# RMS norms of a two-layer trunk on one core: half of the sums by one fp32 product with a matrix of ones

## The reference

```python
def _rmsnorm(x, gain):
    xf = x.astype(jnp.float32)
    y = xf * lax.rsqrt(jnp.mean(xf * xf, axis=-1, keepdims=True) + EPS)
    return (y * gain.astype(jnp.float32)).astype(x.dtype)

def _swiglu(h, w_in, w_out):
    g, u = jnp.split(h @ w_in, 2, axis=-1)
    return (jax.nn.silu(g) * u) @ w_out
```

## Time and profile before

| | |
|---|---|
| median of 3 runs | 2317.88 us |
| the profiled execution | 2317.71 us |
| its span | 2315.6 us |
| TensorE busy | 2298.5 us (99%) |
| VectorE busy | 1600.5 us (69%) |
| ScalarE busy | 979.2 us (42%) |
| granted TensorE clock | 1.00 of full speed |
| HBM read | 245.76 MB |

### The profile page before, as it was taken

How to read it: one execution, slowest core, us unless ns; L and a number is a source line. 1 busy time by engine, 2 the same in 40 slices (tenths; PEclk the granted TensorE clock), 3 DMA queues, 4 the chain that set the end, 5 groups by cost and what they waited for, 6 DMA issues and landing times.

```text
span 2315.6 us, 39357 instructions
## 1 busy us (share of the span) xinstructions
PE 2298.5 (99%) x16336; PEld 2220.4 (96%) x16336; DVE 1600.5 (69%) x2391; ACT 979.2 (42%) x1567; POOL 30.6 (1%) x44
## 2 busy tenths in 40 slices
PE   8999999999999999999999999999999999999999
PEld 8999999988889999999999999999998999999999
DVE  6886776658867876776587767676765668467473
ACT  5433423443656523414364144144545455244242
POOL 0000000000001000000010000000000010000000
PEclk9999999999999999999999999999999999999999
DMA  9352554421101252444215444324133012322122
GB/s 303 128 164 83 190 164 144 148 90 55 58 20 55 92 164 95 143 128 146 92 55 183 128 146 133 105 83 161 55 107 98 19 55 79 104 73 94 58 95 74
DMA packets 200267, 252.89 MB, mean 109 GB/s; under 512 B 13122, under 2 KB 174746, under 8 KB 199962
## 3 DMA queue, kind: packets, MB, share of 16 engines
q1 hardware_dynamic: 199666, 250.20, 32.9%
q10 hardware_dynamic: 424, 0.18, 0.0%
HBM read 245.76 MB, written 3.28 MB: 108 GB/s over the span
## 4 chain that ended last, share of the span: by engine, by line
PE 92%; DVE 3%; ACT 2%; DMA 2%; issue 1%; SPq 1%; POOL 0%; DVEq 0%; ACTq 0%
PE banks L1184 80%; PE banks L1337 1%; PE banks L1514 1%; PE banks L1516 1%; PE banks L1515 1%; DMA w_raw<-ffn_w_in 1%; PE banks L1661 1%; PE banks L1673 1%; PE banks L1688 1%; DMA mod_first<-w_mod 1%; ACT w_hi L2163 1%; DVE w_lo L2885 0%; SPq L1145 0%; SPq L942 0%; DVE w_raw L2906 0%
## 5 line engine op out<-in xcount | busy, mean ns | idle before, releaser
L1184 PE MATMUL banks<-b_hi,w_hi 128*128 128x320 f32 x2496 | 776.8, 311 | 3.7 <-DVE work L3251 2.2
L1184 PE MATMUL banks<-b_hi,w_lo 128*128 128x320 f32 x2496 | 772.4, 309 | 0.0
L1184 PE MATMUL banks<-b_lo,w_hi 128*128 128x320 f32 x2496 | 772.2, 309 | 0.0
L2163 ACT ACTIVATE w_hi<-w_raw 128x1024 fp32r<-128x1024 f32 x317 | 332.5, 1056 | 424.1 <-PE banks L1184 236.2
L2885 DVE TENSOR_TENSOR w_lo<-w_raw,w_hi 128x1024 fp32r<-128x1024 f32 x317 | 387.3, 1224 | 163.4 <-ACT w_hi L2163 161.8
L1184 PEld LDWEIGHTS banks<-b_hi,w_hi 128*128 128x128 f32 x2496 | 468.7, 188 | 16.4 <-issue 10.6
L1184 PEld LDWEIGHTS banks<-b_lo,w_hi 128*128 128x128 f32 x2496 | 468.8, 188 | 0.0
L1184 PEld LDWEIGHTS banks<-b_hi,w_lo 128*128 128x128 f32 x2496 | 468.7, 188 | 0.0
L1184 PE MATMUL banks<-hid_hi,w_hi 128*128 128x320 f32 x1664 | 400.4, 312 | 0.5 <-DVE hid_lo L3189 0.5
L1184 PE MATMUL banks<-hid_hi,w_lo 128*128 128x320 f32 x1664 | 396.6, 309 | 0.0
L1184 PE MATMUL banks<-hid_lo,w_hi 128*128 128x320 f32 x1664 | 396.5, 309 | 0.0
(11 more groups left out here) (383 smaller groups left out, 2422.8 us busy)
## 6 DMA issues: line engine op xcount, KB each, us to landing
w_raw<-ffn_w_in SPq DMA_DIRECT2D x176, 512.0 KB, 4.8
mod_grain<-w_mod SPq DMA_DIRECT2D x78, 512.0 KB, 5.8
w_raw<-ffn_w_out SPq DMA_DIRECT2D x64, 512.0 KB, 4.4
last_grain<-w_mod SPq DMA_DIRECT2D x40, 512.0 KB, 5.1
w_raw<-ffn_w_out SPq DMA_DIRECT2D x32, 384.0 KB, 3.7
w_raw<-w_in_odd SPq DMA_DIRECT2D x20, 512.0 KB, 4.6
mod_first<-w_mod SPq DMA_DIRECT2D x6, 1024.0 KB, 11.8
w_raw<-w_in_even SPq DMA_DIRECT2D x12, 512.0 KB, 6.0
```

What stands on the lines that cost most here:

```text
L1184: ins = pe.matmul(o, w3[w], v3[v][cols], start=first and i == 0, stop=last and i == 2, skip_group_check=onto_read)
L2163: act.activation(ring_in(w_hi, in_slot(f, d, t)), operand(d, t), ACT.Copy).then_inc(hi_ready, 1)
```

## The change

The second half of every norm, and the first half of norms 2 and 5 (`WIDE_FIRST`), take one fp32 product (`wide_sums`): a 128 x 128 matrix of ones as weights and `ss` as the 320 moving columns. It adds over the partitions and leaves each token's sum in all partitions at once. `wide_root` takes the root of 128 x 320 from the bank into `ss`, VectorE inverts it there (`invert_first` all 320 columns, `invert_second` in two parts of 160), and neither the spreading nor the copy is left. For norms 2 and 5 the first sums move in between triples 5 and 6 of the second half of tile 6. The first halves of norms 1, 3 and 4 keep the narrow way; their sums and their spreading both move up by one triple, so that the sums stand ahead of the last triple of tile 6 and the spreading behind the first of tile 7. In `first_double` the second sums stand behind tile 2 instead of tile 1. ScalarE and VectorE orders of the norms are rewritten to match. What is left out of the diff are renamings, the counts that semaphores are waited for, the same lines for norm 4, and `tail_norm` of VectorE, whose new order the rows below it show.

```diff
...
+        WIDE_FIRST = (2, 5)
+        INVERSE_PARTS = 2
...
             def first_double(f, n):
-                plain_parts(f, 0, range(2), range(2))
-                half_sums(n, 1)
-                plain_parts(f, 0, range(2, HK), range(2))
-                spread_inverse(n, 1)
-                plain_parts(f, 0, range(HK, KT), range(2))
+                plain_parts(f, 0, range(3), range(2))
+                wide_sums(n, 1)
+                plain_parts(f, 0, range(3, KT), range(2))
                 plain_parts(f, 1, range(KT), range(2))
...
-            def half_sums(n, hf):
+            def wide_sums(n, hf):
                 pe.wait_ge(square_added, half_squares(n, hf))
+                pe.matmul(spread_of[hf], ones[:, :], ss[:, half_of(hf)], start=True, stop=True).then_inc(sums_ready, 1)
+            def narrow_sums(n):
+                pe.wait_ge(square_added, half_squares(n, 0))
                 for i, (first, _, _) in enumerate(SUM_TILES):
-                    t0 = hf * HALF + first
-                    ins = pe.matmul(token_sums[hf][:, i:i + 1], ss[:, t0:t0 + P], ones[:, 0:1], start=True, stop=True)
+                    ins = pe.matmul(token_sums[:, i:i + 1], ss[:, first:first + P], ones[:, 0:1], start=True, stop=True)
                 ins.then_inc(sums_ready, 1)
-            def spread_inverse(n, hf):
-                pe.wait_ge(inverse_ready, 1 + norms_before(n, hf) + 1)
+            def spread_inverse(n):
+                pe.wait_ge(inverse_ready, inverses_until(n, 0))
                 for i, (first, r0, r1) in enumerate(SUM_TILES):
-                    ins = pe.matmul(inverse_of[hf][:, first + r0:first + r1], rms[r0:r1, hf, i:i + 1].to_broadcast([r1 - r0, P]),
+                    ins = pe.matmul(spread_of[0][:, first + r0:first + r1], rms[r0:r1, i:i + 1].to_broadcast([r1 - r0, P]),
                                     ident[r0:r1, r0:r1], start=True, stop=True)
                 ins.then_inc(inverse_spread, 1)
...
-                out_part(f, c, KT - 2, 1).then_inc(w_used, 1)
-                half_sums(n, 0)
-                out_part(f, c, KT - 1, 1, lambda: spread_inverse(n, 0)).then_inc(w_used, 1)
+                out_part(f, c, KT - 2, 1, {CHUNKS[c] - 1: lambda: narrow_sums(n)}).then_inc(w_used, 1)
+                out_part(f, c, KT - 1, 1, {1: lambda: spread_inverse(n)}).then_inc(w_used, 1)
...
-                part(0, 1).then_inc(out_ready, 1)
-                half_sums(n, 0)
-                part(1, 1, lambda: spread_inverse(n, 0)).then_inc(w_used, 1)
+                part(0, 1, {HK + 1: lambda: wide_sums(n, 0)}).then_inc(out_ready, 1)
+                part(1, 1).then_inc(w_used, 1)
...
-                        half_sums(1, 1)
-                    elif kt == HK - 1:
-                        spread_inverse(1, 1)
+                        wide_sums(1, 1)
...
-            def root(n, hf):
+            def root(n):
+                act.wait_ge(sums_ready, TT + norms_before(n, 0) + 1)
+                act.activation(rms[:, :], token_sums, ACT.Sqrt, scale=1.0 / D, bias=eps[:, 0:1]).then_inc(rms_ready, 1)
+            def wide_root(n, hf):
                 act.wait_ge(sums_ready, TT + norms_before(n, hf) + 1)
-                act.activation(rms[:, hf, :], token_sums[hf], ACT.Sqrt, scale=1.0 / D, bias=eps[:, 0:1])\
+                act.activation(ss[:, half_of(hf)], spread_of[hf], ACT.Sqrt, scale=1.0 / D, bias=eps[:, 0:1])\
                     .then_inc(rms_ready, 1)
-            def keep_inverse_of(n, hf):
-                act.wait_ge(inverse_spread, 2 * n + hf + 1)
-                act.activation(ss[:, half_of(hf)], inverse_of[hf], ACT.Copy).then_inc(inverse_kept_in[hf], 1)
...
-                root(n, 0)
-                square_half(n, KT - 2, 1, x_before)
-                for kt in range(2):
-                    after_first(kt)
+                if n in WIDE_FIRST:
+                    wide_root(n, 0)
+                    after_first(0)
+                    square_half(n, KT - 2, 1, x_before)
+                    for kt in (1, 2):
+                        after_first(kt)
+                else:
+                    root(n)
+                    square_half(n, KT - 2, 1, x_before)
+                    for kt in range(2):
+                        after_first(kt)
                 square_half(n, KT - 1, 1, x_before)
...
                 tail_squares(n, x_before, between, lambda kt: form_high(n, f, kt, 0))
-                for kt in range(2, HK):
+                for kt in range(3 if n in WIDE_FIRST else 2, HK):
                     form_high(n, f, kt, 0)
-                root(n, 1)
+                wide_root(n, 1)
                 item_hi(f, 0, 2)
                 form_high(n, f, HK, 0)
                 item_hi(f, 0, 3)
                 for kt in range(HK + 1, KT):
                     form_high(n, f, kt, 0)
-                    if kt == HK + 1:
-                        keep_inverse_of(n, 1)
...
-            def invert(n, hf):
-                dve.wait_ge(rms_ready, 1 + norms_before(n, hf) + 1)
-                dve.reciprocal(rms[:, hf, :], rms[:, hf, :]).then_inc(inverse_ready, 1)
+            def invert(n):
+                dve.wait_ge(rms_ready, 1 + norms_before(n, 0) + 1)
+                dve.reciprocal(rms[:, :], rms[:, :]).then_inc(inverse_ready, 1)
+            def invert_first(n):
+                dve.wait_ge(rms_ready, 1 + norms_before(n, 0) + 1)
+                dve.reciprocal(ss[:, half_of(0)], ss[:, half_of(0)]).then_inc(inverse_ready, 1)
+            def invert_second(n, part):
+                if part == 0:
+                    dve.wait_ge(rms_ready, 1 + norms_before(n, 1) + 1)
+                cols = slice(HALF + part * HALF // INVERSE_PARTS, HALF + (part + 1) * HALF // INVERSE_PARTS)
+                dve.reciprocal(ss[:, cols], ss[:, cols]).then_inc(inverse_ready, 1)
             def scale_half(n, view, kts, hf):
-                if n == 0 or hf == 1:
-                    dve.wait_ge(inverse_kept_in[hf], n + 1 if hf == 1 else 1)
+                narrow = n > 0 and hf == 0 and n not in WIDE_FIRST
+                if n == 0:
+                    dve.wait_ge(inverse_kept_in[hf], 1)
+                elif narrow:
+                    dve.wait_ge(inverse_spread, spreads_until(n))
                 else:
-                    dve.wait_ge(inverse_spread, 2 * n + 1)
-                inverse = ss[:, half_of(hf)] if n == 0 or hf == 1 else inverse_of[hf]
+                    dve.wait_ge(inverse_ready, inverses_until(n, hf))
+                inverse = spread_of[hf] if narrow else ss[:, half_of(hf)]
...
                 tail_norm(n, last_half, scale, low, middle)
-                invert(n, 1)
-                scale_form(n, f, slice(6, 8), 0)
+                scale(slice(6, 8), 0)
+                invert_second(n, 0)
                 item_lo(f, 0, 2)
                 low(slice(4, 5), 0)
                 item_lo(f, 0, 3)
                 low(slice(5, 6), 0)
+                invert_second(n, 1)
                 scale(slice(0, 2), 1)
                 low(slice(6, 8), 0)
...
```

More of the change, by code:

```diff
@@ L116, in trunk @@
         den = place("den", [P, C_HEADS])
-        rms = place("rms", [P, 2, len(SUM_TILES)])
+        rms = place("rms", [P, len(SUM_TILES)])
         x_rms = place("x_rms", [P, TT])
@@ L152, in trunk @@
         SUM_BANK = (6, 7)
-        token_sums = [bank[b][:, HALF:HALF + len(SUM_TILES)] for b in SUM_BANK]
-        inverse_of = [bank[b][:, 0:HALF] for b in SUM_BANK]
+        token_sums = bank[SUM_BANK[0]][:, HALF:HALF + len(SUM_TILES)]
+        spread_of = [bank[b][:, 0:HALF] for b in SUM_BANK]
         consts_in = sem("consts_in")
@@ L1490, in tail_pair, with part @@
                 pe.wait_ge(lo_ready, unit + 1)
-                def part(i, hf, midway=None):
+                def part(i, hf, steps={}):
                     for k in range(KT):
-                        if midway is not None and k == 2:
-                            midway()
+                        if k in steps:
+                            steps[k]()
                         ins = split_product([(bank[TAIL_BANKS[i][hf]][:, 0:HALF], (slice(None), k, half_of(hf)))],
```

69 lines of the change are left out of this document (44 added, 25 removed).

## The result

The changed kernel takes 2328.51 us (median of 6 runs, 2327.02 to 2330.61), the kernel before 2317.99 (6 runs): ratio 1.0049, 95% interval 1.0039 to 1.0059, 10.5 us slower. Forecast were 2323.5 and a range up to 2327.0. The sign and, but for sizes, the waits in the norms came out; the total didn't.

What follows compares the result with a forecast made beforehand. TensorE, busy 99% of the span, was taken as the bound; 6.6 us less work was outweighed by waits. Norm costs of 1.1 + 1.1 + 1.5 + 1.5 + 0.6 = 5.8 us on 2317.7 gave 2323.5, range 2315.5 to 2327.

Steps and rivals of the forecast that it cites:

- Prices of the operations: Reciprocal 1.14 us for 160 columns, 2.14 for 320; root 0.44; wide product 0.73.
- the 6.6 of the forecast: TensorE's work: each of seven wide halves saves 0.94 us, 6.6 us in all.
- First half of norms 2 and 5: Tile 0 of norm 2 starts at 721.75 instead of 722.18, 0.4 us won.
- The 0.25 added for Pool: Norm 2, first half: 0.25 us added for Pool's shift waiting out VectorE's second scale.
- Tile 4 and tile 6: Norm 2: TensorE waits 1.5 us, tile 4 at 731.1, tile 6 at 735.5; costs 1.1, norm 5 the same.
- From there on VectorE does two tiles in 2.1 us and TensorE in 3.5, so the second half of the tokens hides the rest: Norm 2 from tile 6 on: VectorE's remaining work is hidden, so no further cost; norm 5 the same.
- Norms 1, 3 and 4: Cost 1.5, 1.5 and 0.6 us; tile 0 starts 0.5 late in norms 1 and 4, unchanged in norm 3.
- The sum: Norm costs 1.1 + 1.1 + 1.5 + 1.5 + 0.6 = 5.8 us, added to 2317.7 give 2323.5.
- A: Rival: reciprocal cheap past 50 columns (0.6 us for 160 or less); 2.6 us in all, 2320.3; chance 0.29.
- B: Rival, faster: shorter chain behind the moved sums lets the 6.6 us of saved work land; 2313.0; chance 0.12.
- C: Rival, worse: long reciprocals shut Pool out, tiles 6 and 7 0.5 to 1 us later; 2325.5; chance 0.09.

Runs made afterwards that it cites:

- E3: Changed kernel with the first halves of norms 2 and 5 summed, inverted and spread the narrow way at their old places: 2328.94 us, ratio 1.0050.
- E2: Changed kernel with the second halves' wide sums back behind tile 1 in norms 2, 3 and 5: 2324.30 us, ratio 1.0032.
- E1: Changed kernel with each long reciprocal cut to two columns, the other columns left uninverted: 2323.12 us, ratio 1.0026.
- E5: Changed kernel with both parts of the second half's reciprocal later in VectorE's order: 2335.40 us, ratio 1.0078.
- E4: Changed kernel with the narrow first sums and spreading of norms 1, 3 and 4 back at their old places: 2327.88 us, ratio 1.0043.
- E9: Changed kernel, unchanged but for an empty line, profiled a second time: 2326.29 us.
- E14: Changed kernel with 60 more TensorE instructions (15 fp32 products of 8 columns) ahead of the first product: 2330.55 us, ratio 1.0061.
- E15: Kernel before with 196 more TensorE instructions (49 fp32 products of 8 columns) ahead of the first product: 2336.95 us, ratio 1.0090.
- E8: Kernel before, unchanged but for an empty line, profiled a second time: 2316.82 us.
- E10: Changed kernel with wide sums only in norms 2, 3, 5, second ones behind tile 1, narrow sums at old places: 2318.03 us, ratio 1.0007.
- E16: E10's kernel with 40 more TensorE instructions (10 fp32 products of 8 columns) ahead of the first product: 2319.71 us, ratio 1.0012.

## Why the prediction was wrong

- **Prices of the operations: the reciprocal right, the others off a little.** Root 0.09 dearer. The wide product has two instructions 0.27 apart as forecast, but the 0.19 for the way back to fp32r isn't there: 0.54, so by this price TensorE saves 1.3 us more over the seven halves than the 6.6 of the forecast, and the waits give back more than the totals show. By the repeat count of 8 in the Trainium skill (VectorE: DVE Perf Modes, "First, the fixed hardware budget") I had estimated 1.5 us for 160 columns; the trace has 1.15, so the straight line of the rows was the better guide.
- **First half of norms 2 and 5: right.** The changed kernel comes into norm 2 0.5 us late; less that, tile 0 starts at 721.57 (forecast 721.75). E3 prices the gain at 0.5. The 0.25 added for Pool wasn't needed: its shift had begun before VectorE's second scale and took 0.45.
- **Tile 4 and tile 6: right.** Wait 1.62 (forecast 1.5), and less the 0.5, tile 4 at 730.99 (731.1), tile 6 at 735.46 (735.5). E2 shows the cause, E1 that the reciprocal isn't the part that binds there.
- **"From there on VectorE does two tiles in 2.1 us and TensorE in 3.5, so the second half of the tokens hides the rest": wrong**, 0.3 us in norms 2, 3 and 5, lost near 763 of norm 2, and E5 shows how steep it gets (2.1 us when VectorE's scales of the second half come another 2 us later).
- **Norms 1, 3 and 4: mis-sized.** The earlier narrow sums cost 0.68 in norms 1 and 4 (E4), not 0.5; in norm 3 they cost nothing, as forecast. Norm 3 is 1.7 late at tile 6, not 1.5, before the 0.4 of the second half of the tokens. All norms: 7.9 us in E9 instead of 5.8.
- **The sum: this is the step that failed.** "2317.7 + 5.8" takes it that untouched parts cost what they did, and gives no reason. They cost 2.7 us more in E9 and 6.0 in the first profile after. With the norms' 7.9 alone the sum would be 2325.6, 2.1 over the forecast; most of the rest up to 2328.51 is here. Parts 2 and 3 I haven't taken apart. Shown by E14, E15 and the load near 905 for part 1: TensorE has 20 instructions less for each wide half, its 33221 instructions arrive in 129 pieces (some 257 each), and the pieces fall into other loads. The Trainium skill (Runtime: NRT & Kernel Launch, "Instruction fetch mechanics") says that code comes in 16 KiB blocks of 256 instructions over a DMA queue of the engine's own, and that the cost of a boundary is mostly hidden. The trace agrees with the blocks (129 fetches of 16 KB); the cost isn't hidden from the load beside it, which near 905 takes 6.1 to 6.7 us instead of 4.8 to 5.3.
- **A stretch at half clock** was missing too. In the first profile after, 12 matmuls of norm 3 stand 0.27 apart instead of 0.147, right behind the waits of 1.62 and 0.22. The windows (us, busy and count of each engine, granted clock, DMA share, GB/s):

```profile
1160.00:1184.00 24.00, 21.78 (x143) 20.44 (x142) 16.43 (x31) 13.95 (x26) 4.38 (x8) 1.00 0.15 45
1184.00:1188.00 4.00, 4.00 (x19) 4.00 (x18) 3.38 (x5) 3.04 (x7) 0.00 (x0) 0.57 0.78 240
1188.00:1225.00 37.00, 37.00 (x254) 37.00 (x253) 33.64 (x36) 25.90 (x39) 0.00 (x0) 1.00 0.11 33
```

It costs 0.6 us in norm 3 (2.72 against 2.15), 0.65 in norm 5 of E3, 1.6 in norm 1 of E14. Five profiles have one behind a norm's wait, all behind a wait of 1.5 us or more; E9, E1 and E2 among others have such waits and no stretch. That the wait is its condition is argued, not shown.
- **Rivals.** A's world was built in E1, whose norms cost 2.65 where A said 2.6. B's condition, w_lo within 2.5 us of the sums, wasn't met: 3.5. C fell: beside a reciprocal Pool's shift took 0.45 us, not over a microsecond.

Open is why the load near 216 lands late in four profiles (before, E8, E1, E10) and not in seven others with a fetch at the same place, 206.9 to 207.5, just ahead of its issue. Near 1363 only the first profile of the changed kernel has a late load, and its fetch stands where E9's does. In part 3, a load issued at 2099.0 takes 5.3 to 6.1 us in the profiles with a fetch at 2099 or just before, and 4.8 in before and E8, with the fetch at 2109; but E16's takes 7.75 (a wait of 1.84 at 2108), with the fetch well ahead of it. No version beat the kernel before.
